# Two heads of a pair, one after the other or by turns: the order of half-width matmuls in a two-block transformer step

## The chip, the core and the metric

The kernel is one program on one NeuronCore of a Trainium2 chip. The metric is the device time of one execution in microseconds (us). The kernel before takes 2046.39 us, the median of 3 runs (2043.55 to 2046.69). One execution was also taken down by the hardware profiler; all rows below come from it.

Five engines work side by side, each through its own list of instructions, and wait for one another through semaphores. TensorE (PE in the rows) multiplies matrices, VectorE (DVE), ScalarE (ACT) and GpSimd (POOL) do the rest, SyncE (SP) issues the DMAs of the weights. PEld is TensorE's weight load: a matmul instruction takes a stationary operand (loaded first) and streams a moving operand past it. All data here are fp32, and each fp32 matmul of the program shows up in the trace as two matmul records with a weight load each. They are called passes here: one matmul is two passes.

## The reference

Two blocks run in sequence on 256 tokens of width 1024. The first has two layers, with multi-head latent attention (8 heads, value width 64) beside a Fourier and a convolution branch, then an MLP. The second mixes an RWKV-7 branch (8 heads of 64), an S5 branch and a gated linear attention (GLA, 4 heads with keys of 64), then cross-attention and a gated MLP. The parts that matter here:

```
attention      o[h] = softmax(q[h] k[h]^T * scale) v[h]              h = 0..7, value width 64
GLA            u_c = (k * exp(b_last - b))^T v, o = mask(q k^T) v + q S     4 heads, chunks of 64 tokens
RWKV-7 step    S = S*w + (S . -kk) (kk*a)^T + v k^T;  y = S . r             8 heads, state 64x64
```

The kernel computes RWKV in chunks of 64 tokens: per head and chunk, products of 64x64 blocks and the inverse of a unit triangular 64x64 block (built up from products), then a chain over the four chunks.

## The kernel before, in words

**Halves.** Everything is stored with features on the 128 partitions. A head is 64 wide, so a pair of heads fills the partitions: head 2i sits on partitions 0 to 63 (`hh = 0`), head 2i+1 on 64 to 127 (`hh = 1`). A product of one head therefore uses half of TensorE's array. A 64x64 block matmul reads partitions 0-63 and writes 0-63 of a PSUM bank, or reads 64-127 and writes 64-127. Values times probabilities of the attention (`pv`) reads all 128 partitions (keys) and writes only 64.

**The order.** The program is written out by hand; each engine follows the order of the code. PSUM has 8 banks. `open_bank` takes the next of a pool in turn and waits until the engine that read its last contents has freed it. `taken(pe, key)` makes TensorE wait for that reader, `did(..., key=...)` is its signal.

**Attention** (TensorE's part from line 706). Steps go over (pair i, head hh, query tile qt). In layer 0 there are 4 query tiles of 128, two with 256 keys and two with 512, so 32 steps; in layer 1 there are 2 tiles, both with 512 keys, so 16 steps. In step j TensorE computes the scores of j; DVE takes the maximum, ACT the exponential, DVE the reciprocal, and POOL scales the probabilities (line 1582). Three steps later (LAG = 3) TensorE transposes them (line 719), ACT copies the result to one of 3 slots of `probT` (line 1312), and one step after that TensorE multiplies values by probabilities: 2 or 4 matmuls of 64 columns of weights with 128 moving columns. In layer 0, TensorE also computes modulation blocks in between (`mod_block`, weights of 32 columns, each k in another quarter of the partitions of one bank).

**GLA** (from line 887): transposes of the values of each head (`gvt`), block products (`blocks`, line 896) and the updates `gu`, between projection tiles of the RWKV branch.

**RWKV** (from line 1020): `product(name, lhs, rhs)` (line 1027) calls `blocks` for each half of the four pairs: 2 halves of a name, 16 matmuls of 64x64 each, first the 8 of `hh = 0` and then the 8 of `hh = 1`. There are 21 products after the block transposes `vt`. Between them stand gate tiles (`gate_tiles`, 8 full matmuls each), which need nothing from the chain. DVE or ACT copies each half out. Then comes the chain over 4 chunks, `rx`, `ru`, a gate tile, `rs`, `ry`: TensorE waits for DVE after `rx` (line 2152), `ru` and `rs` (line 2164).

Of the kernel before, what the change touches and what calls it, by code (L numbers as in the profile page):

```python
# [27 lines left out]
P = 128  # L28
# [22 lines left out]
CHUNK = 64  # L51
# [21 lines left out]
LAG = 3  # L73
# [208 lines left out]
def two_blocks(nc, weights, vectors, table_in, x_in, ctx_in, mem_in, c_in, s5b_in, s5c_in, out):  # L282
# [3 lines left out]
    with ExitStack() as ctx:  # L286
# [228 lines left out]
        def steps(l):  # L515
            q_tiles = range(4) if l == 0 else range(2, 4)
            return [(i, hh, qt) for i in range(HEADS // 2) for hh in range(2) for qt in q_tiles]
# [18 lines left out]
        def _(pe):  # L536
# [91 lines left out]
            for l in range(LAYERS):  # L628
# [71 lines left out]
                for j in range(len(todo) + LAG + 1):  # L700
# [23 lines left out]
                    if 0 <= j - LAG - 1:  # L724
                        t = j - LAG - 1
                        i, hh, qt = todo[t]
                        key = ("pv", l, i)
                        if t % (len(todo) // 4) == 0:
                            open_bank(key, "hold")
                            if t == 0:  # L730
# [156 lines left out]
            for i in range(2):  # L887
                key = ("gvt", i)
                o_ = open_bank(key)
                for hh in range(2):  # L890
                    for c in range(NCH):
                        mm(o_[64 * hh:64 * hh + 64, c * P:(c + 1) * P], g_v[:, 2 * i + hh, c * CHUNK:(c + 1) * CHUNK],
                           table("ident"), True, True, key if hh == 1 and c == NCH - 1 else None)
            pe.wait_ge(S["gla_dve"], 3)

            def blocks(key, lhs, rhs, tiles, skip=()):

                o_ = open_bank(key)
                for hh in range(2):
                    hp = slice(64 * hh, 64 * hh + 64)  # L900
                    for n, i in enumerate(tiles):
                        for c in range(NCH):
# [10 lines left out]
            for i in range(2):  # L913
                taken(pe, ("gvt", i))
                key = ("gu", i)
                o_ = open_bank(key)
                for hh in range(2):
                    hp = slice(64 * hh, 64 * hh + 64)
                    for c in range(NCH - 1):
                        mm(o_[hp, c * P:(c + 1) * P], g_ket[hp, i, c * CHUNK:(c + 1) * CHUNK], g_vt[hp, i, c, :], True, True,  # L920
                           key if hh == 1 and c == NCH - 2 else None)
# [157 lines left out]
            def heads():  # L1079
                for hh in range(2):  # L1080
                    for i in range(4):
                        yield slice(64 * hh, 64 * hh + 64), i, hh == 1 and i == 3
            for c in range(NCH):
# [5 lines left out]
                for hp, i, end in heads():  # L1089
                    oo = o_[hp, 64 * i:64 * i + 64]  # L1090
                    if c:
                        mm(oo, r_kk[hp, i, cc], r_s[hp, i, :], True, False)
                    mm(oo, r_m2[hp, i, cc], r_vt[hp, i, cc], c == 0, True, key if end else None)
# [3 lines left out]
                for hp, i, end in heads():  # L1097
                    mm(o_[hp, 64 * i:64 * i + 64], c_tt[hp, i, cc], r_x[hp, i, :], True, True, key if end else None)
                gate_tiles(1)
                taken(pe, ("ru", c))  # L1100
                if c < NCH - 1:
                    key = ("rs", c)
                    o_ = open_bank(key)
                    for hp, i, end in heads():
                        oo = o_[hp, 64 * i:64 * i + 64]
# [4 lines left out]
                for hp, i, end in heads():  # L1110
                    oo = o_[hp, 64 * i:64 * i + 64]
                    if c:
                        mm(oo, r_s[hp, i, :], r_rt[hp, i, cc], True, False)
                    mm(oo, r_u[hp, i, :], r_n1[hp, i, cc], c == 0, False)
                    mm(oo, r_vt[hp, i, cc], r_n2[hp, i, cc], False, True, key if end else None)
# [1218 lines left out]
```

How the kernel before makes its waits and increments, by code:

```python
        def finished(eng, key):  # L476
            b, n = plan[key]
            eng.wait_ge(bank_full[b], n)
# [1 line left out]
        def taken(eng, key):  # L481
            b, n = plan[key]
            eng.wait_ge(bank_free[b], n)
# [8 lines left out]
            def did(ins, name=None, key=None, wait=True):  # L493
                s = bank_free[plan[key][0]] if key is not None else S[name or order]
                at_key = ("bank", plan[key][0]) if key is not None else (name or order)
                ins.then_inc(s, 1)
                if wait:
                    if key is not None:
                        eng.wait_ge(s, plan[key][1])
                    else:
                        count[at_key] = count.get(at_key, 0) + 1
                        eng.wait_ge(s, count[at_key])
                elif key is None:
                    count[at_key] = count.get(at_key, 0) + 1
                return ins
# [13 lines left out]
        def s5_turned_back(eng, n):  # L519
            if n % 4 == 3:
                eng.wait_ge(S["s5_states_v"], (n + 1) // 4)
            else:
                eng.wait_ge(S["s5_states"], n + 1 - (n + 1) // 4)
# [10 lines left out]
        @block.tensor  # L535
# [6 lines left out]
            def open_bank(key, pool="run"):  # L542
                b = pools[pool][turn[pool] % len(pools[pool])]
                turn[pool] += 1
                if uses[b]:
                    pe.wait_ge(bank_free[b], uses[b])
                uses[b] += 1
                plan[key] = (b, uses[b])
                return ps[:, b, :]
# [423 lines left out]
            s5_in(0)  # L973
            s5_in(1)
            pe.wait_ge(S["s5_dve"], 4)
```

## Time and profile before

| | us |
|---|---|
| median of 3 runs | 2046.39 |
| profiled execution | 2042.25 |
| its span | 2040.1 |
| TensorE busy | 1919.9 (94% of the span) |
| DVE / ACT / POOL busy | 911.9 / 411.6 / 230.9 |
| TensorE's share of the chain that ended last | 82% |

The profiled execution lies 4.1 us under the median. The stages that the change touches are the attention of layer 0 (180 to 289 us of the span) and of layer 1 (844 to 889), the GLA products (1228 to 1263), and the RWKV products and chain (1450 to 1625). The granted clock of TensorE is 0.964 of full speed on average.

### The profile page before, as it was taken

The page shows a single profiled execution, that of the slowest core. Times are in us where ns is not written, and L with a number is a line of the kernel's source. Part 1 is how long each engine was busy: PE and PEld are TensorE (multiplying, and loading weights), DVE is VectorE, ACT ScalarE, POOL GpSimd, SP SyncE. Part 2 cuts the span into 40 slices and gives each one's busy share as a digit, 9 for nine tenths or more (in the row PEclk, how much of TensorE's full clock was granted, in tenths as well). Part 3 has the DMA queues.
Part 4 walks back from the last instruction along what each step waited for, and adds up shares of the span by engine and source line. Part 5 has one row for each costly group of instructions (what it writes and reads, how often), then busy time and mean ns, then how long its engine had stood idle before and what let it go on. Part 6 is the DMA issues. An engine that isn't in the chain of part 4 may idle for free.

```text
span 2040.1 us, 26345 instructions
## 1 busy us (share of the span) xinstructions
PE 1919.9 (94%) x10716; PEld 1511.7 (74%) x10716; DVE 911.9 (45%) x1729; ACT 411.6 (20%) x778; POOL 230.9 (11%) x244
## 2 busy tenths in 40 slices
PE   6998999899999998999999899788999989999997
PEld 2444554788888886578999788544898878788886
DVE  1364322645754337637865312755610152245521
ACT  3124441320121103542210022102211001210000
POOL 0002420121012000322410000342000000000000
PEclk8999999999999999999999999887899999999999
DMA  8642641123332222124444542232212144244443
GB/s 314 256 186 106 260 174 62 63 101 105 124 104 83 83 83 104 42 85 143 166 165 164 176 152 94 76 103 105 82 43 84 42 165 145 83 145 145 161 149 103
DMA packets 38417, 256.23 MB, mean 126 GB/s; under 512 B 4097, under 2 KB 7169, under 8 KB 8609
## 3 DMA queue, kind: packets, MB, share of 16 engines
q1 hardware_dynamic: 35808, 239.80, 33.7%
q0 software_dynamic: 1920, 10.62, 1.4%
q10 hardware_dynamic: 576, 4.19, 0.5%
q8 instruction: 85, 1.39, 0.3%
q14 instruction: 28, 0.22, 0.0%
HBM read 247.26 MB, written 7.34 MB: 125 GB/s over the span
## 4 chain that ended last, share of the span: by engine, by line
PE 82%; DVE 10%; ACT 3%; issue 2%; DMA 1%; POOL 1%; SPq 0%; ACTq 0%; DVEq 0%; POOLq 0%
PE ps L567 82%; DVE arena L1779 1%; DVE arena L1935 1%; PE ps L719 1%; DMA cs_raw<-c_t 0%; DVE aux L1807 0%; DVE arena L1808 0%; DVE arena L1809 0%; ACT hT L1239 0%; DVE spare L2059 0%; ACT aux L1215 0%; DMA kept_keys_values<-arena 0%; DMA ring<-weights 0%; DVE aux L1722 0%; DVE aux L1718 0%
## 5 line engine op out<-in xcount | busy, mean ns | idle before, releaser
L567 PE MATMUL ps<-hT,ring 128*128 128x256 f32 (+3 forms) x3184 | 746.2, 393 | 24.0 <-issue 17.0
L567 PEld LDWEIGHTS ps<-hT,ring 128*128 128x128 f32 (+1 forms) x3184 | 579.0, 195 | 172.3 <-issue 97.5
L567 PE MATMUL ps<-arena,ring 128*128 128x256 f32 (+3 forms) x1756 | 359.1, 360 | 5.7 <-DVE arena L1809 3.2
L567 PEld LDWEIGHTS ps<-arena,ring 128*128 128x128 f32 (+1 forms) x1756 | 296.2, 192 | 58.4 <-issue 15.2
L567 PE MATMUL ps<-arena,sums 128*128 128x256 f32 (+1 forms) x768 | 136.5, 327 | 1.3 <-DVE aux L1873 1.3
L567 PEld LDWEIGHTS ps<-arena,sums 128*128 128x128 f32 x768 | 118.2, 191 | 12.3 <-DVE aux L1873 2.5
L567 PE MATMUL ps<-arena 64*64 64x64 f32 (+3 forms) x1392 | 92.7, 241 | 3.0 <-DVE arena L2111 1.6
L567 PEld LDWEIGHTS ps<-arena 64*64 64x64 f32 (+2 forms) x1392 | 86.6, 148 | 9.4 <-issue 6.4
L1193 ACT ACTIVATE aux<-xT 128x256 f32<-128x256 f32 (+1 forms) x64 | 30.9, 494 | 295.9 <-DVE xT L1965 98.6
L1582 POOL TENSOR_SCALAR aux<-aux,small 128x512 f32<-128x512 f32 (+1 forms) x48 | 71.3, 1491 | 152.9 <-DVE small L1825 152.9
L567 PE MATMUL ps<-hT,sums 128*128 128x128 f32 (+1 forms) x512 | 78.9, 302 | 0.7 <-DVE aux L1873 0.4
L567 PE MATMUL ps<-aux,tab 128*128 128x256 f32 (+1 forms) x156 | 59.3, 496 | 21.5 <-ACT aux L1193 17.7
L1849 DVE TENSOR_TENSOR sums<-ring 128x512 f32<-128x512 f32 x64 | 44.1, 690 | 71.5 <-PE ps L567 70.4
L1600 POOL TENSOR_TENSOR arena<-arena 128x256 f32<-128x256 f32 (+1 forms) x32 | 27.0, 844 | 426.9 <-ACT arena L1356 426.9
L1779 DVE SCALAR_TENSOR_TENSOR arena<-arena,vec 128x512 f32<-128x512 f32 (+1 forms) x120 | 73.6, 614 | 3.2
L567 PEld LDWEIGHTS ps<-hT,sums 128*128 128x128 f32 x512 | 70.1, 193 | 4.7 <-DVE aux L1873 0.8
L1818 DVE TENSOR_REDUCE small<-ps 128x1 f32<-128x512 f32 (+1 forms) x48 | 28.9, 602 | 99.6 <-PE ps L567 99.1
L1355 ACT ACTIVATE arena<-arena 128x1024 f32<-128x1024 f32 (+1 forms) x32 | 27.0, 844 | 209.8 <-DVE arena L1881 209.8
L1404 ACT ACTIVATE arena<-ps 128x512 f32<-128x512 f32 (+2 forms) x56 | 28.1, 501 | 181.6 <-PE ps L567 181.4
L567 PE MATMUL ps<-spare,ring 128*128 128x256 f32 x256 | 60.6, 379 | 1.3 <-DVE spare L1915 1.3
L567 PEld LDWEIGHTS ps<-aux,tab 128*128 128x128 f32 x156 | 29.4, 195 | 39.1 <-DMA cs_raw<-c_t 14.8
L567 PE MATMUL ps<-spare,sums 128*128 128x256 f32 x256 | 57.9, 379 | 0.0
(335 smaller groups left out, 2042.6 us busy)
## 6 DMA issues: line engine op xcount, KB each, us to landing
ring<-weights SPq DMA_DIRECT2D x224, 1024.0 KB, 4.9
kept_turns<-aux ACTq DMA_DIRECT2D x4, 1024.0 KB, 5.6
arena<-kept_turns POOLq DMA_DIRECT2D x6, 512.0 KB, 4.3
kept_keys_values<-arena POOLq DMA_DIRECT2D x1, 2048.0 KB, 6.6
arena<-kept_keys_values POOLq DMA_DIRECT2D x1, 2048.0 KB, 8.1
tab<-tables SPq DMA_DIRECT2D x1, 1411.5 KB, 10.9
xT<-ctx_t SPq DMA_DIRECT2D x1, 1024.0 KB, 6.0
xT<-x_t SPq DMA_DIRECT2D x1, 1024.0 KB, 8.2
```

The source lines that it names most:

```text
L567: ins = nc.tensor.matmul(o_, lhsT, rhs, start=start, stop=stop, skip_group_check=True)
L719: ins = nc.tensor.transpose(o_[:, kt * P:(kt + 1) * P], prob[:, t % 4, kt * P:(kt + 1) * P], table("ident"))
L1193: did(f(sq[:, k, s], xT[:, k, s], ACT.Square), "squares", wait=False)
L1355: did(f(two, two, ACT.Relu))
L1404: did(f(dst, bank(key)[0:m, 0:n], func, **kw), key=key, wait=wait)
L1582: did(nc.gpsimd.tensor_scalar(prob[:, t % 4, 0:nk], prob[:, t % 4, 0:nk], small[:, 3, t:t + 1], None, ALU.mult), "prob_ready", wait=False)
L1600: did(nc.gpsimd.tensor_tensor(t1, b12, b11, ALU.subtract))
L1779: did(v.scalar_tensor_tensor(dst, src, w, dst, ALU.mult, ALU.add), name)
L1818: did(v.reduce_max(small[:, 2, j:j + 1], bank(("s", l, j))[:, 0:nk], AX))
L1849: did(tt(s3, a11, a21, ALU.subtract))
L1935: did(v.reciprocal(a, a))
```

## The change

The same matmuls are issued, with the same operands and in the same number; only their order on TensorE changes.

- In `blocks`, `gvt`, `gu` and the RWKV chain the loop over the half moves inside, so that matmuls of partitions 0-63 and 64-127 alternate. In the chain, where a block is a sum of two or three products, the matmuls of one product alternate first, then those of the next. The group `go`, which writes all 128 partitions, stays.
- In the attention the steps go over (pair, query tile, head). Values times probabilities is done once for two steps, at the second, and its matmuls alternate between the two heads.

```diff
-            return [(i, hh, qt) for i in range(HEADS // 2) for hh in range(2) for qt in q_tiles]
+            return [(i, hh, qt) for i in range(HEADS // 2) for qt in q_tiles for hh in range(2)]
...
-                    if 0 <= j - LAG - 1:
-                        t = j - LAG - 1
-                        i, hh, qt = todo[t]
+                    t = j - LAG - 1
+                    if t >= 0 and t % 2 == 1:
+
+                        i, _, qt = todo[t]
...
+                        taken(pe, ("t", l, t - 1))
                         taken(pe, ("t", l, t))
-                        last = t % (len(todo) // 4) == len(todo) // 4 - 1
                         for kt in range(key_tiles(qt)):
-                            h = 2 * i + hh
                             end = kt == key_tiles(qt) - 1
-                            mm(o_[64 * hh:64 * hh + 64, qt * P:(qt + 1) * P], vtok[:, kt, h * DV:(h + 1) * DV],
-                               probT[:, t % 3, kt * P:(kt + 1) * P], kt == 0, end, key if last and end else None)
+                            for hh in range(2):
+                                h = 2 * i + hh
+                                mm(o_[64 * hh:64 * hh + 64, qt * P:(qt + 1) * P], vtok[:, kt, h * DV:(h + 1) * DV],
+                                   probT[:, (t - 1 + hh) % 3, kt * P:(kt + 1) * P], kt == 0, end,
+                                   key if t % per == per - 1 and end and hh else None)
...
             def blocks(key, lhs, rhs, tiles, skip=()):
 
                 o_ = open_bank(key)
-                for hh in range(2):
-                    hp = slice(64 * hh, 64 * hh + 64)
-                    for n, i in enumerate(tiles):
-                        for c in range(NCH):
-                            cc = slice(c * CHUNK, (c + 1) * CHUNK)
+                for n, i in enumerate(tiles):
+                    for c in range(NCH):
+                        cc = slice(c * CHUNK, (c + 1) * CHUNK)
+                        for hh in range(2):
+                            hp = slice(64 * hh, 64 * hh + 64)
...
-                    for hp, i, end in heads():
-                        oo = o_[hp, 64 * i:64 * i + 64]
-                        mm(oo, r_a2t[hp, i, cc], r_u[hp, i, :], True, False)
-                        mm(oo, r_k2t[hp, i, cc], r_vt[hp, i, cc], False, True, key if end else None)
+                    for i in range(4):
+                        v_ = slice(64 * i, 64 * i + 64)
+                        for hp in half_rows:
+                            mm(o_[hp, v_], r_a2t[hp, i, cc], r_u[hp, i, :], True, False)
+                        for hp in half_rows:
+                            mm(o_[hp, v_], r_k2t[hp, i, cc], r_vt[hp, i, cc], False, True,
+                               key if i == 3 and hp is half_rows[1] else None)
```

`gvt`, `gu`, `rx`, `ru` and `ry` are changed in the same way.

The order on TensorE in the attention of layer 1, three steps before; `spare,arena` are scores, `tab,aux` transposes, `aux,arena` values times probabilities of one head:

```order
L567 MATMUL ps<-spare,arena 128x512
L719 MATMUL ps<-tab,aux 128x128 x4
L567 MATMUL ps<-aux,arena 64x128 x4
L567 MATMUL ps<-spare,arena 128x512
L719 MATMUL ps<-tab,aux 128x128 x4
L567 MATMUL ps<-aux,arena 64x128 x4
```

And four steps of the changed kernel at the same place:

```order
L567 MATMUL ps<-spare,arena 128x512
L719 MATMUL ps<-tab,aux 128x128 x4
L567 MATMUL ps<-spare,arena 128x512
L719 MATMUL ps<-tab,aux 128x128 x4
L567 MATMUL ps<-aux,arena 64x128 x8
L567 MATMUL ps<-spare,arena 128x512
```

The four matmuls after each step's transposes have become eight after every second step's.

In the RWKV chain, on TensorE at the start of `rs` of the first chunk, before; `rinv,spare` is a2t times u, `spare` is k2t times v, both of one head:

```order
L567 MATMUL ps<-hT,ring 128x256 x8
L567 MATMUL ps<-rinv,spare 64x64
L567 MATMUL ps<-spare 64x64
L567 MATMUL ps<-rinv,spare 64x64
L567 MATMUL ps<-spare 64x64
```

And now:

```order
L567 MATMUL ps<-hT,ring 128x256 x8
L567 MATMUL ps<-rinv,spare 64x64 x2
L567 MATMUL ps<-spare 64x64 x2
L567 MATMUL ps<-rinv,spare 64x64 x2
L567 MATMUL ps<-spare 64x64 x2
```

The x2 is one matmul for each half. Where both products have the same names, as in `blocks`, the rows read alike before and after and are not shown.

## Rows read from the trace of the kernel before

**Rows 1.** The page: busy time, granted clock in 40 slices, the chain that ended last.

```profile
PE 1919.9 (94%) x10716; PEld 1511.7 (74%) x10716; DVE 911.9 (45%) x1729; ACT 411.6 (20%) x778; POOL 230.9 (11%) x244
...
PEclk8999999999999999999999999887899999999999
...
PE 82%; DVE 10%; ACT 3%; issue 2%; DMA 1%; POOL 1%; SPq 0%; ACTq 0%; DVEq 0%; POOLq 0%
```

**Rows 2.** Matmul groups by shape: busy us, mean ns; idle time before, releaser.

```profile
L567 PE MATMUL ps<-arena 64*64 64x64 f32 x1248 | 68.2, 230 | 1.6 <-DVE arena L2111 1.6
...
L567 PE MATMUL ps<-aux,arena 128*64 128x128 f32 x320 | 45.6, 283 | 1.5 <-ACT aux L1312 1.5
```

**Rows 3.** TensorE in time, attention of layer 1: start us, us, instructions merged.

```profile
859.72 1.12 PE L567 MATMUL ps<-spare,arena 96*128 96x512 f32 x2
860.68 0.60 PE L719 MATMUL ps<-tab,aux 128*128 128x128 f32 x4
861.21 1.09 PE L567 MATMUL ps<-aux,arena 128*64 128x128 f32 x8
862.23 1.13 PE L567 MATMUL ps<-spare,arena 96*128 96x512 f32 x2
```

**Rows 4.** TensorE in time, attention of layer 0.

```profile
222.60 0.65 PE L567 MATMUL ps<-aux,arena 128*64 128x128 f32 x4
223.18 1.13 PE L567 MATMUL ps<-spare,arena 96*128 96x512 f32 x2
224.24 1.92 PE L567 MATMUL ps<-ring,cs 128*32 128x512 f32 x16
...
286.68 0.63 PE L719 MATMUL ps<-tab,aux 128*128 128x128 f32 x4 [0.33 <-POOL aux L1582]
```

**Rows 5.** POOL in time, attention of layer 1.

```profile
864.63 1.72 POOL L1582 TENSOR_SCALAR aux<-aux,small 128x512 f32<-128x512 f32 x1 [0.80 <-DVE small L1825]
```

**Rows 6.** Counts of matmul records in two stretches of `gvt`: one stream, then two.

```profile
1227.94:1228.16 0.22, 0.22 (x4) 1.00 0.00 0
1228.27:1228.49 0.22, 0.22 (x7) 1.00 0.94 112
```

**Rows 7.** TensorE in time, GLA: `gvt`, a projection tile, `gu`, a projection tile.

```profile
1227.68 2.57 PE L567 MATMUL ps<-tab,arena 128*64 128x128 f32 x32
...
1233.51 10.63 PE L567 MATMUL ps<-hT,ring 128*128 128x256 f32 x48
...
1244.07 1.79 PE L567 MATMUL ps<-arena 64*64 64x128 f32 x24
1245.79 10.63 PE L567 MATMUL ps<-hT,ring 128*128 128x256 f32 x48
```

**Rows 8.** TensorE in time, RWKV products and gate tiles.

```profile
1455.32 11.10 PE L567 MATMUL ps<-arena 64*64 64x64 f32 x128 [1.64 <-DVE arena L2111]
1466.36 5.13 PE L567 MATMUL ps<-hT,ring 128*128 128x256 f32 x16
1471.41 6.42 PE L567 MATMUL ps<-arena 64*64 64x64 f32 x128
1477.76 3.72 PE L567 MATMUL ps<-hT,ring 128*128 128x256 f32 x16
```

**Rows 9.** TensorE in time, where product `m2` ends and `a2t` begins.

```profile
1484.48 0.22 PE L567 MATMUL ps<-arena 64*64 64x64 f32 x1
1484.54 0.22 PE L567 MATMUL ps<-tab,arena 64*64 64x64 f32 x1
1484.54 0.22 PE L567 MATMUL ps<-arena 64*64 64x64 f32 x1
1484.60 0.22 PE L567 MATMUL ps<-tab,arena 64*64 64x64 f32 x1
```

**Rows 10.** TensorE in time, RWKV chain: `rx` of the third chunk, then `ru`.

```profile
1599.74 0.28 PE L567 MATMUL ps<-rinv,arena 64*64 64x64 f32 x2
1599.85 0.28 PE L567 MATMUL ps<-spare 64*64 64x64 f32 x2
...
1601.71 1.12 PE L567 MATMUL ps<-rinv,arena 64*64 64x64 f32 x16 [0.59 <-DVE rinv L2152]
```

**Rows 11.** Busy us by engine, then granted clock, DMA share, GB/s.

```profile
1456.00:1466.00 10.00, 10.00 (x120) 10.00 (x120) 3.46 (x5) 0.00 (x0) 0.00 (x0) 0.50 0.01 3
```

**Rows 12.** ACT and DVE copying halves of products out of PSUM.

```profile
1494.86 0.60 ACT L1404 ACTIVATE spare<-ps 128x512 f32<-128x512 f32 x1 [0.91 <-PE ps L567]
...
1523.42 0.69 DVE L2140 TENSOR_TENSOR arena<-ps,tab 128x512 f32<-128x512 f32 x1 [14.79 <-PE ps L567]
```

More of the change, by code:

```diff
@@ L723, in _ @@
                         mod_turn(1, MOD_STEP[j])
-                    if 0 <= j - LAG - 1:
-                        t = j - LAG - 1
-                        i, hh, qt = todo[t]
+                    t = j - LAG - 1
+                    if t >= 0 and t % 2 == 1:
+                        i, _, qt = todo[t]
                         key = ("pv", l, i)
-                        if t % (len(todo) // 4) == 0:
+                        per = len(todo) // 4
+                        if t % per == 1:
                             open_bank(key, "hold")
-                            if t == 0:
+                            if t == 1:
                                 for tt in range(4):
@@ L898, in blocks @@
                 o_ = open_bank(key)
-                for hh in range(2):
-                    hp = slice(64 * hh, 64 * hh + 64)
-                    for n, i in enumerate(tiles):
-                        for c in range(NCH):
-                            cc = slice(c * CHUNK, (c + 1) * CHUNK)
+                for n, i in enumerate(tiles):
+                    for c in range(NCH):
+                        cc = slice(c * CHUNK, (c + 1) * CHUNK)
+                        for hh in range(2):
+                            hp = slice(64 * hh, 64 * hh + 64)
                             end = hh == 1 and i == tiles[-1] and c == NCH - 1
@@ L916, in _ @@
                 o_ = open_bank(key)
-                for hh in range(2):
-                    hp = slice(64 * hh, 64 * hh + 64)
-                    for c in range(NCH - 1):
+                for c in range(NCH - 1):
+                    for hh in range(2):
+                        hp = slice(64 * hh, 64 * hh + 64)
                         mm(o_[hp, c * P:(c + 1) * P], g_ket[hp, i, c * CHUNK:(c + 1) * CHUNK], g_vt[hp, i, c, :], True, True,
@@ L1076, in _ @@
                     taken(pe, (name, half))
[L1079 to L1082, printed above, removed]
+            half_rows = (slice(0, 64), slice(64, 128))
             for c in range(NCH):
@@ L1096, in _ @@
                 o_ = open_bank(key)
-                for hp, i, end in heads():
-                    mm(o_[hp, 64 * i:64 * i + 64], c_tt[hp, i, cc], r_x[hp, i, :], True, True, key if end else None)
+                for i in range(4):
+                    for hp in half_rows:
+                        mm(o_[hp, 64 * i:64 * i + 64], c_tt[hp, i, cc], r_x[hp, i, :], True, True,
+                           key if i == 3 and hp is half_rows[1] else None)
                 gate_tiles(1)
@@ L1103, in _ @@
                     o_ = open_bank(key)
-                    for hp, i, end in heads():
-                        oo = o_[hp, 64 * i:64 * i + 64]
-                        mm(oo, r_a2t[hp, i, cc], r_u[hp, i, :], True, False)
-                        mm(oo, r_k2t[hp, i, cc], r_vt[hp, i, cc], False, True, key if end else None)
+                    for i in range(4):
+                        v_ = slice(64 * i, 64 * i + 64)
+                        for hp in half_rows:
+                            mm(o_[hp, v_], r_a2t[hp, i, cc], r_u[hp, i, :], True, False)
+                        for hp in half_rows:
+                            mm(o_[hp, v_], r_k2t[hp, i, cc], r_vt[hp, i, cc], False, True,
+                               key if i == 3 and hp is half_rows[1] else None)
                 key = ("ry", c)
                 o_ = open_bank(key)
-                for hp, i, end in heads():
-                    oo = o_[hp, 64 * i:64 * i + 64]
+                for i in range(4):
+                    v_ = slice(64 * i, 64 * i + 64)
                     if c:
-                        mm(oo, r_s[hp, i, :], r_rt[hp, i, cc], True, False)
-                    mm(oo, r_u[hp, i, :], r_n1[hp, i, cc], c == 0, False)
-                    mm(oo, r_vt[hp, i, cc], r_n2[hp, i, cc], False, True, key if end else None)
+                        for hp in half_rows:
+                            mm(o_[hp, v_], r_s[hp, i, :], r_rt[hp, i, cc], True, False)
+                    for hp in half_rows:
+                        mm(o_[hp, v_], r_u[hp, i, :], r_n1[hp, i, cc], c == 0, False)
+                    for hp in half_rows:
+                        mm(o_[hp, v_], r_vt[hp, i, cc], r_n2[hp, i, cc], False, True,
+                           key if i == 3 and hp is half_rows[1] else None)
             gate_tiles(1)
```

4 lines of the change are left out of this document (2 added, 2 removed).

## The prediction

> **What bounds the kernel now.** I read the page first: TensorE is busy 94% of the span and makes 82% of the chain that ended last [rows 1]. So what TensorE no longer does comes off the time, unless a wait takes its place. Then the groups by shape: the change touches the 64x64 block matmuls and the 64-column ones of the attention, and TensorE is idle before either for less than 2 us in all [rows 2]. The sums below use start-to-start distances from the timeline, because a record's length (230 or 283 ns) holds a pipeline tail that the next record overlaps.
>
> What matters is the pace of one pass in a half of the array. In the attention of layer 1, 8 passes of values times probabilities take 862.23 - 861.21 = 1.02 us [rows 3]; in layer 0, 4 passes take 0.58 [rows 4]. The difference is 0.44 for 4 passes, so 0.109 us per pass and 0.15 us to get in and out. For 64x64 blocks, where two operands alternate in one half, 2 passes take 0.115 us [rows 10], so 0.058 per pass. But 128 passes of two products take 1477.76 - 1471.41 = 6.35 us, only 0.050 each [rows 8]. Where one product ends and the next begins, the records say why: passes of `arena` (the old, partitions 64-127) and `tab,arena` (the new, partitions 0-63) start in the same 0.06 us [rows 9]. The two halves run side by side, but only near a change of half. A run of 128 passes changes half 7 times. All in one line it would be 128 x 0.058 + 0.14 = 7.6 us; 6.35 is 1.26 less, 0.18 (three passes) at each of the 7. Three changes alone, those to another bank, would have given 7.06, so the overlap exists within a bank too. For columns alone `gvt` shows it: 4 records in 0.22 us, then 7 in 0.22 us [rows 6]; and the modulation block, four strips of 32 columns in one bank, does 16 passes of 512 columns in 1.92 us [rows 4], while a pass of 512 alone takes about 0.43 (two of them and a change make 1.13, of which the change is some 0.1 and the tail 0.16 [rows 3]).
>
> **The change part by part.** It removes no matmul. It lets each pass of one half find its partner of the other beside it all the time, since about three waiting passes are looked past and a partner is now at most two behind.
>
> *Attention, layer 1.* Two steps now hold two groups of 8 passes, 2.04 us. Afterwards one group of 16 passes in 8 slots: 8 x 0.109 + 0.15 = 1.02. Saved 1.02 for each of 8 pairs: 8.2 us. The next engine is POOL with 1.72 us per step [rows 5] against 2.51 of TensorE (862.23 - 859.72 = 2.51 [rows 3]); TensorE's step becomes 2.0, so POOL keeps hidden.
>
> *Attention, layer 0.* 8 pairs of long tiles at 1.02 and 8 of short ones at 0.58: 12.8 us. The steps go by tile now, so four short ones follow each other; the modulation blocks lie at the same steps, at least one in any three, and cover the probabilities' chain.
>
> *Tails.* The last transposes of layer 0 already wait 0.33 us for POOL [rows 4], so what is saved between the last scores and there turns into waiting: half of the 16 passes in between and a bit, 1.1 us. Layer 1 has no such wait but some 0.5 us of reserve; I take 0.5 lost. Attention in sum: 8.2 + 12.8 - 1.6 = 19.4 us.
>
> *GLA.* `gvt` with the two `blocks` behind it takes from 1227.68 to 1233.51, 5.83 us for 32 passes with 128 moving columns and 64 with 64 [rows 7]. Afterwards 16 x 0.109 + 32 x 0.058 + 0.35 for the changes = 3.95: 1.9 saved. `gu` goes from 1.72 (1245.79 - 1244.07) to 12 x 0.109 + 0.15 = 1.46: 0.3 saved. Nothing waits there. 2.1 us.
>
> *`vt`.* TensorE waits 1.64 us for DVE (line 2111) right behind it [rows 8]; what `vt` saves (1.2) lengthens this wait. 0.
>
> *Products.* Ten runs of 128 passes, each followed by a gate tile, and one of 64. A run becomes 64 x 0.058 + 0.14 = 3.9: 2.47 saved, ten times, and 1.3 for the short one: 26.0 us. The first run goes at a granted clock of 0.50 [rows 11], the level of 1.2 GHz, and takes 11.04 us (1466.36 - 1455.32 [rows 8]); in slots of 0.107 it is 7.1 or so, which gives 0.9 more than counted, taking part of the first gate tile into account. Against that stand new waits. A product half now comes every 0.95 us instead of 1.5, and 0.43 + 0.60 us pass from its end until ACT has copied it, 0.49 + 0.69 for DVE. The copy of `k2t`'s second half begins at 1494.86, that half ending at 1494.43 [rows 12]. A product that reads the one directly before it starts its first half when that copy is done, 0.95 after the end of the half: `d2` after `k2t` waits some 0.2, `r` after `d8` and `tt` after `ft` some 0.35 each. 0.9 lost. The copies themselves (0.60, 0.69) fit in 0.95. In sum 26.0 us.
>
> *Chain.* 448 passes. Where TensorE waits at the end (after `rx` of 32 passes, three times) the last pass comes 0.75 sooner, after 16 passes 0.28 sooner (`rx` once, `ru` four times); `rs` saves 0.57 three times and `ry` 0.75 once and 1.04 three times: 2.25 + 1.4 + 1.7 + 3.9 = 9.2 us. The wait of 0.59 for line 2152 [rows 10] is latency and stays.
>
> *Sum.* 19.4 + 2.1 + 0 + 26.0 + 9.2 = 56.7 us. The profiled execution takes 2042.25, its span 2040.1 and 2.15 around it; it goes to 1985.5. It lies 4.1 under the median of the runs, 2046.39, so the median goes to 1989.7. I say 1989.5.
>
> **A rule against it.** The Trainium skill, TensorEngine Tiling (Array Packing), section Restrictions and Gotchas, says that different row tiles write to different PSUM banks and cannot use one bank at the same time. The changed blocks let both halves write one bank, on other partitions. By that rule the two halves would have to run one after the other, and the 64x64 parts would get slower than now. The trace disagrees so far: the 6.35 us of a run need overlap at the changes within a bank too. It shows three passes at a time, not a steady stream, so the rule has its chance in the second rival.
>
> **Rivals.**
>
> *A. The passes are not fed fast enough (10%).* The longest stretch that the trace shows holds 0.050 us per pass, weight load included [rows 8]; the change wants 0.029. If the supply ended at 0.050, columns alone would gain (19.4 + 0.9, their pace is 0.055 per pass): 2046.4 - 20.3 = 2026. With a supply of 0.040 about half of the other 36 us remains: 2008. For it: no long stretch is faster. Against it: near each change two passes start every 0.058. The skill's TensorE: Matmul & The Clock Gate (section Wait — 56ns, not 53.3ns?) gives a floor of about 25 ns from start to start however small the matmul. That floor would leave all of the sum, 0.029 being above it.
>
> *B. Alternating halves run in line (4%).* If overlap needs some rest (another bank, or a half that has just drained), every pass costs its own 0.058: 1920 passes at 0.058 instead of 0.050 are 15 us more, and values times probabilities saves only its 24 ways in and out, 3.6: about 2058. If each turn also costs the unhidden first load (the first record of a run is 0.27 long, the others 0.22 [rows 9, 8]), 960 turns at 0.05 bring 48 more: about 2106. It decides from the point where a turn costs more than the three passes of overlap, 0.18, spread over 8 matmuls. Against it: rows 6 and 9.
>
> *C. The clock (4%).* The first product run and its gate tile go at 0.50 [rows 8, 11]. The engine had waited 1.64 us before. Shorter bursts between the same waits of the chain could bring more such stretches; 10 to 20 us at half pace cost 5 to 10: 1997. It can also go the other way: if a denser stream is granted full clock sooner, the 16 us from 1455 shrink by up to 6: 1984.
>
> *D. The attention keeps its pace (2%).* POOL, DVE's taps or the weights of the modulation blocks become the bound: half of 19.4 goes, 1999.
>
> **How the numbers follow.** The forecast holds 80%, with its own range of 1980 to 2000 for the waits and the clock. To leave out no more than 2 in 10 the range takes in the sooner clock and the half-way of A: 1976 to 2012. About 0.2% can be told from no change here. Faster by more than that are the forecast, A, C and D: 96%. B has the rest: no change 1%, where a partial overlap just meets the lost pace, slower 3%.
>
> **What would show it.** In the profile after: in layer 1 a group of 16 `aux,arena` passes per two steps from start to start 1.0 us, and 4.0 us for two steps; after each gate tile 128 passes in 3.9 us; `gu` in 1.5; the wait for line 2111 longer (2.8 us); new waits of 0.2 to 0.4 us on ACT line 1404 and DVE line 2140 between products; the stages 180 to 289, 844 to 889 and 1450 to 1625 shorter by about 12, 8 and 35 us. Runs of 128 passes that take over 5 us would prove A or B; the same runs at full pace with a granted clock of 0.50 over more than 25 us of that stage, C.

## The result, and the profile after

The changed kernel takes 1988.51 us, the median of 4 runs (1983.68 to 1990.18), against 2045.3 (2043.55 to 2046.69) for the kernel before in the same session: a ratio of 0.9719, 95% interval 0.9699 to 0.9739. A second set of runs gave 1985.36 and 0.9706 (0.9688 to 0.9724). The forecast was 1989.5 us, the ratio that it stood for 0.972.

The page of the profiled execution, answering to [rows 1]:

```profile
span 1981.5 us, 26361 instructions
...
PE 1850.5 (93%) x10716; PEld 1447.1 (73%) x10716; DVE 911.4 (46%) x1729; ACT 411.2 (21%) x778; POOL 230.4 (12%) x244
...
PE 81%; DVE 11%; ACT 3%; issue 2%; DMA 1%; POOL 1%; SPq 0%; ACTq 0%; DVEq 0%; POOLq 0%
```

TensorE has as many instructions as before, is busy 69.4 us less and still makes four fifths of the chain that ended last. The groups by shape, answering to [rows 2]:

```profile
L567 PE MATMUL ps<-arena 64*64 64x64 f32 x1248 | 40.5, 223 | 3.0 <-DVE arena L2124 3.0
...
L567 PE MATMUL ps<-aux,arena 128*64 128x128 f32 x320 | 22.9, 280 | 8.7 <-ACT aux L1325 8.7
```

One record is hardly shorter than before (223 ns for 230, 280 for 283), but the busy time of both groups falls by 41 to 50%, as passes of the two halves lie side by side. The third column holds the one surprise: before the groups of values times probabilities TensorE now waits 8.7 us for ACT's copy of the transposes (line 1325, line 1312 before), where it waited 1.5.

TensorE in time at the RWKV products (answers to [rows 8]):

```profile
1440.96 5.18 PE L567 MATMUL ps<-arena 64*64 64x64 f32 x128 [2.97 <-DVE arena L2124]
1446.08 3.72 PE L567 MATMUL ps<-hT,ring 128*128 128x256 f32 x16
1449.73 3.95 PE L567 MATMUL ps<-arena 64*64 64x64 f32 x128
1453.61 3.72 PE L567 MATMUL ps<-hT,ring 128*128 128x256 f32 x16
...
1487.56 4.09 PE L567 MATMUL ps<-arena 64*64 64x64 f32 x128
1491.58 3.72 PE L567 MATMUL ps<-hT,ring 128*128 128x256 f32 x16
```

A run of 128 passes goes from 6.35 us to 1453.61 - 1449.73 = 3.88, or 30 ns per pass. The run that holds a product reading the one just before it takes 1491.58 - 1487.56 = 4.02. The wait ahead of the first run is 2.97 us, as `vt` gets done sooner and DVE (line 2124) doesn't.

And in the attention of layer 1 (answers to [rows 3]), with ACT in the same stretch below it:

```profile
856.27 1.09 PE L567 MATMUL ps<-aux,arena 128*64 128x128 f32 x16 [0.89 <-ACT aux L1325]
857.30 1.12 PE L567 MATMUL ps<-spare,arena 96*128 96x512 f32 x2
858.26 0.60 PE L719 MATMUL ps<-tab,aux 128*128 128x128 f32 x4
858.70 1.02 PE L567 MATMUL ps<-spare,arena 96*128 96x512 f32 x2
859.56 0.60 PE L719 MATMUL ps<-tab,aux 128*128 128x128 f32 x4
861.05 1.09 PE L567 MATMUL ps<-aux,arena 128*64 128x128 f32 x16 [0.89 <-ACT aux L1325]
```

```profile
859.50 0.69 ACT L1317 ACTIVATE aux<-ps,small 128x512 f32<-128x512 f32 x1 [1.88 <-DVE small L1832]
860.09 0.19 ACT L1317 ACTIVATION_READ_ACCUMULATOR aux<-ps,small 128x1 f32 x1
860.31 0.60 ACT L1325 ACTIVATE aux<-ps 128x512 f32<-128x512 f32 x1
861.00 0.69 ACT L1317 ACTIVATE aux<-ps,small 128x512 f32<-128x512 f32 x1
```

The group of 16 passes takes the forecast 1.03 us (857.30 - 856.27). But two steps take 861.05 - 856.27 = 4.78 us and not 4.0. The transposes that line 1325 copies at 860.31 had been written by 858.86. ACT ran its work in the order of the code here, and ahead of that copy the code has the exponential of a later step (line 1317, at 859.50), which waits for DVE's maximum of scores that TensorE has only just computed. DVE at that place:

```profile
858.53 0.69 DVE L1831 TENSOR_REDUCE small<-ps 128x1 f32<-128x512 f32 x1 [1.82 <-PE ps L567]
859.25 0.15 DVE L1832 TENSOR_SCALAR small<-small 128x1 f32<-128x1 f32 x1
```

So the way from TensorE through DVE and ACT back to TensorE is: scores from 857.30, maximum at 858.53, exponential at 859.50, copy at 860.31, values times probabilities at 861.05, in all 3.75 us. TensorE's own work in that time is 2.86 us (861.05 - 857.30 - 0.89). In the kernel before a group of 1.02 us more lay in it, so that way stayed hidden.

The time by stages, in us of the span. A stage's half-clock time is in brackets: how long the granted clock stood at 0.50, the level of 1.2 GHz, within it. "Attention" ends where TensorE goes on to something else; "RWKV products" begin with `vt`. The second profiled execution of the changed kernel is shown too.

| stage | before | after | after, again | forecast of the gain |
|---|---|---|---|---|
| up to the first scores | 180.6 | 182.2 | 182.0 | 0 |
| attention, layer 0 | 108.4 (3.4) | 99.9 (10.2) | 97.9 (3.4) | 11.7 |
| between the attentions | 555.6 | 559.6 | 555.6 | 0 |
| attention, layer 1 | 43.9 (3.4) | 39.6 (0) | 40.4 (3.4) | 7.7 |
| up to `gvt` | 339.2 | 338.8 | 339.3 | 0 |
| GLA products | 17.9 | 15.7 | 15.7 | 2.1 |
| S5, up to `vt` | 204.7 (61.4) | 200.1 (47.8) | 206.8 (64.9) | 0 |
| RWKV products | 125.8 (13.7) | 95.4 (3.4) | 95.7 (3.4) | 26.0 |
| RWKV chain | 48.4 (10.2) | 35.6 (3.4) | 35.7 (3.4) | 9.2 |
| rest | 415.6 | 414.5 | 414.6 | 0 |

Between the two executions of the same program only the clock differs, by 4 us between the attentions and by 6.7 in S5. Against the second, whose clock in the attention is that of before, the gain is 10.5 + 3.5 there, 2.2 in GLA and 42.8 in RWKV; the other stages are 2.5 us longer in sum (S5 by 2.1, with 3.5 us more at half clock), which makes the 56.5 us between the spans (2040.1 and 1983.6).

Two things stand to be explained: 5.4 us that the attention didn't give (14.0 for 19.4), and 7.6 us that RWKV gave beyond its 35.2.

### The profile page after: what moved, and what is told of

It is laid out like the page before. It is cut to its first block, busy times and chain, and to the rows that moved or that the text cites. A ratio compares the mean times of both kernels' runs of the same rounds, so it can differ in the third digit from the quotient of the medians.

```text
span 1981.5 us, 26361 instructions
## 1 busy us (share of the span) xinstructions
PE 1850.5 (93%) x10716; PEld 1447.1 (73%) x10716; DVE 911.4 (46%) x1729; ACT 411.2 (21%) x778; POOL 230.4 (12%) x244
## 3 DMA queue, kind: packets, MB, share of 16 engines
q1 hardware_dynamic: 35808, 239.80, 34.8%
## 4 chain that ended last, share of the span: by engine, by line
PE 81%; DVE 11%; ACT 3%; issue 2%; DMA 1%; POOL 1%; SPq 0%; ACTq 0%; DVEq 0%; POOLq 0%
PE ps L567 80%; DVE arena L1792 1%; DVE arena L1948 1%; DMA ring<-weights 1%; DVE small L1831 1%; DMA cs_raw<-c_t 0%; DVE aux L1820 0%; DVE arena L1821 0%; DVE arena L1822 0%; ACT hT L1252 0%; ACT aux L1228 0%; PE ps L719 0%; DVE spare L2072 0%; DMA kept_keys_values<-arena 0%; POOL aux L1595 0%
## 5 line engine op out<-in xcount | busy, mean ns | idle before, releaser
L567 PE MATMUL ps<-arena 64*64 64x64 f32 (+3 forms) x1392 | 63.6, 233 | 4.3 <-DVE arena L2124 3.0
L567 PEld LDWEIGHTS ps<-arena 64*64 64x64 f32 (+2 forms) x1392 | 57.5, 143 | 10.9 <-issue 6.4
L567 PE MATMUL ps<-spare,ring 128*128 128x256 f32 x256 | 61.4, 383 | 2.1 <-DVE spare L1928 2.1
L567 PEld LDWEIGHTS ps<-aux,tab 128*128 128x128 f32 x156 | 30.4, 201 | 40.3 <-DMA cs_raw<-c_t 14.7
L1888 DVE TENSOR_TENSOR aux<-aux,ps 128x256 f32<-128x256 f32 x24 | 10.1, 421 | 106.8 <-PE ps L567 106.6
```

Of the source, the lines that this page charges most:

```text
L567: ins = nc.tensor.matmul(o_, lhsT, rhs, start=start, stop=stop, skip_group_check=True)
L1888: did(tt(u2, p1, product("p6"), ALU.add))
```

## The experiments

### Each part alone

`attn_only` is the kernel before with the change of the attention, `blocks_only` has the other part (blocks, `gvt`, `gu`, chain). `after_again` is the changed kernel, for a second time. In the two cuts of code, minus lines are those of the changed kernel and plus lines those of the kernel named.

```diff
--- attn_only against after
-                for n, i in enumerate(tiles):
-                    for c in range(NCH):
-                        cc = slice(c * CHUNK, (c + 1) * CHUNK)
-                        for hh in range(2):
+                for hh in range(2):
+                    for n, i in enumerate(tiles):
+                        for c in range(NCH):
...
--- blocks_only against after
-            return [(i, hh, qt) for i in range(HEADS // 2) for qt in q_tiles for hh in range(2)]
+            return [(i, hh, qt) for i in range(HEADS // 2) for hh in range(2) for qt in q_tiles]
...
```

> Only the attention part of the change; blocks, gvt, gu and chain in the order of before. My theory: the attention saves what the two profiles show, about 8.5 us in layer 0 and 2 to 4 in layer 1, because TensorE waits for ACT's copy of the transposes (line 1312) some 0.9 us before each double group in layer 1. So 2033 to 2036 us. The pass pace in a double group is 0.055 us or less. Rival, the prediction's sizes: 19.4 us, 2026. If the MLP behind it slows down because the attention got denser, less than 8 us remain and the MLP stretch between the two attentions is 4 us longer than before.

Measured: 2034.1 us, ratio 0.9943 (0.9921 to 0.9965). This median describes no run: of the 8, four took 2027.7 to 2028.6 us at a mean granted clock of 0.964, and four 2039.6 to 2041.0 at 0.956 or 0.957. Only one of the first four was profiled, so in which stage the others lost their 12 us is open. That 2034.1 lies within the expected 2033 to 2036 is luck. In the profiled execution layer 0 takes 97.9 us and layer 1 40.4, all other stages what they take in the kernel before, within 0.6; its attention saves 14.0 us, more than the 10.5 to 12.5 expected.

> Only the 64x64 blocks, gvt, gu and the chain alternate; attention as before. My theory: 37 us by the sum of slots (2.1 GLA, 26.0 products, 9.2 chain) and up to 8 more where the stretch of halved clock at the start of the products does not appear: 2000 to 2008 us. A run of 128 passes takes 3.88 us. Rival: the 8 us more are not of the clock but of the blocks themselves; then the stage from vt to the chain's end takes 131 us even in a profile that shows a granted clock of 0.5 there.

Measured: 2000.02 us, ratio 0.9768 (0.9751 to 0.9784). GLA 15.7, RWKV products 95.8, chain 35.6, the attention as before (108.4 and 44.0). The time is at the lower end of the expected 2000 to 2008.

> The changed kernel again, on the chip and in the rounds of the three others. 0.972 of before. A stretch of halved clock of 3.4 us at the start of the RWKV products if its length goes with the order of the blocks, anything between 0 and 14 us if it is chance.

Measured: 1985.36 us, with the half-clock stretch of 3.4 us. The parts add up in the spans of the profiled executions: 2040.1 - 2025.6 = 14.5 us for the attention and 2040.1 - 1998.0 = 42.1 for the rest make 56.6, the whole has 2040.1 - 1983.6 = 56.5. (The ratios of the medians add up as well, 0.0057 + 0.0232 = 0.0289 for 0.0294, but the first of them is that of no run.) So the parts don't disturb one another, and the attention's shortfall is its own: 97.9 and 40.4 us stand in `attn_only` too.

### What the attention waits for

Theory: ACT's order. The copy of the transposes stands behind an exponential that isn't due yet, and TensorE's shorter step lays that bare. `act_first` puts the copy first (but for layer 0's steps with a modulation block). `pv_later` leaves ACT alone and does the double group one step later, ahead of the transposes of that step, so that the copy has a step more. Rival: another engine (POOL, or DVE) sets the step, and the copy only shows it.

```diff
--- act_first, ACT's part of one step
-                    if j < len(todo):
-                        ...
-                        did(f(prob[:, j % 4, 0:nk], bank(("s", l, j))[:, 0:nk], ACT.Exp, ...), key=("s", l, j))
                     ...
                     if j >= LAG:
                         t = j - LAG
                         nk = key_tiles(todo[t][2]) * P
                         finished(act, ("t", l, t))
                         did(f(probT[:, t % 3, 0:nk], bank(("t", l, t))[:, 0:nk], ACT.Copy), key=("t", l, t))
+                    if not mods_here:
+                        exps()
--- pv_later, TensorE's part of one step (the transposes now come behind this)
-                    t = j - LAG - 1
+                    t = j - LAG - 2
                     if t >= 0 and t % 2 == 1:
                         ...
```

> The changed kernel, with ACT copying the transposes before it takes the exponential of the same step (except in steps with a modulation block). My theory: the wait before the double group came from the copy standing behind the exponential, so it vanishes in layer 1 (5.7 us over 7 times) and in the steps of layer 0 without a modulation block; two steps take 4.0 to 4.1 us instead of 4.78; 5 to 8 us faster than the changed kernel, 1981 to 1984. Rival: POOL and DVE bind at 2.3 us per step anyway; then the wait moves to POOL line 1582 and no more than 2 us come of it.

> The changed kernel, with values times probabilities one step later, ahead of that step's transposes; ACT's order is unchanged. My theory: there are then 3.97 us of TensorE's work between the scores and the group that needs the copy behind them, against 3.8 us of chain, so the wait for ACT goes as well, and two steps take 4.0 us in layer 1; 5 to 8 us faster than the changed kernel, less some 1 us at the end of each layer. Rival: as for act_first, POOL binds at 2.3 us per step.

Measured: `act_first` 1983.34 us, ratio 0.9689 (0.9671 to 0.9707); `pv_later` 1978.95 us, 0.9667 (0.9651 to 0.9684). The changed kernel has 0.9706 (0.9688 to 0.9724), which `act_first` still overlaps and `pv_later` just doesn't. By these ratios the gains are 3.5 and 8.0 us, where 5 to 8 were expected of either (of `pv_later` less 1 for its ends). `act_first` falls short by its ratio, though its 1983.34 lies within the expected 1981 to 1984; its profile has 8.5 us more at half clock in layer 0 than `pv_later`. What decides is the stage and the wait itself. TensorE in time in layer 1, first of `act_first`, then of `pv_later`:

```profile
855.70 1.09 PE L567 MATMUL ps<-aux,arena 128*64 128x128 f32 x16
856.72 1.12 PE L567 MATMUL ps<-spare,arena 96*128 96x512 f32 x2
857.68 0.60 PE L719 MATMUL ps<-tab,aux 128*128 128x128 f32 x4
858.12 1.02 PE L567 MATMUL ps<-spare,arena 96*128 96x512 f32 x2
858.99 0.60 PE L719 MATMUL ps<-tab,aux 128*128 128x128 f32 x4
859.52 1.09 PE L567 MATMUL ps<-aux,arena 128*64 128x128 f32 x16
```

```profile
848.77 1.09 PE L567 MATMUL ps<-aux,arena 128*64 128x128 f32 x16
849.80 0.66 PE L740 MATMUL ps<-tab,aux 128*128 128x128 f32 x4
850.29 1.02 PE L567 MATMUL ps<-spare,arena 96*128 96x512 f32 x2
...
852.55 1.09 PE L567 MATMUL ps<-aux,arena 128*64 128x128 f32 x16
```

And POOL in `pv_later`, the scaling of the probabilities:

```profile
848.82 3.47 POOL L1595 TENSOR_SCALAR aux<-aux,small 128x512 f32<-128x512 f32 x2 [0.51 <-DVE small L1838]
852.59 3.25 POOL L1595 TENSOR_SCALAR aux<-aux,small 128x512 f32<-128x512 f32 x2 [0.30 <-DVE small L1838]
```

Two steps are 859.52 - 855.70 = 3.82 us in the one and 852.55 - 848.77 = 3.78 in the other. The wait on ACT's copy is gone between these steps in both; over the whole kernel it falls from 8.7 us to 1.9 and 2.0. POOL does its two steps in 3.25 to 3.47 us and still idles between them, though only for 0.3 to 0.5. So the rival falls: no other engine held the step at 4.78. In this table, us of the stage, in brackets the half-clock time, then TensorE's idle time in it:

| | layer 0 | idle | layer 1 | idle |
|---|---|---|---|---|
| before | 108.4 (3.4) | 7.6 | 43.9 (3.4) | 2.6 |
| after, again | 97.9 (3.4) | 11.8 | 40.4 (3.4) | 7.7 |
| act_first | 99.2 (11.9) | 9.9 | 36.6 (3.4) | 4.2 |
| pv_later | 93.5 (3.4) | 8.6 | 34.8 (0) | 4.0 |
| both | 93.1 (3.4) | 8.1 | 36.1 (3.4) | 3.9 |

With the wait out of the way the attention gives 24.0 us (`pv_later`; 23.1 with both), more than the 19.4 forecast, with the stage's half-clock time 3.4 us less in the first and as before in the second. The forecast had allowed only 1.6 for tails and waits; it had no place for a way through another engine's order.

That the gain exceeds even the 21.0 us that the forecast had before tails has a second source. It put TensorE's own work of two steps at 5.02 - 1.02 = 4.0 us, and it is 3.8. Where scores now follow the transposes directly, they start 0.44 us after them (858.12 - 857.68) and the next transposes 0.87 after that; before, it was 0.53 from transposes to values and 0.96 from scores to transposes ([rows 3]). There are fewer changes of shape, and that is 0.18 us for each pair of steps, 1.4 in layer 1. The rest of the surplus wasn't taken apart.

`pv_later_act_first` has both edits, `before_act_first` only ACT's, on the kernel before.

> Both repairs of the attention: values times probabilities one step later, ahead of the transposes, and ACT's copy before its exponential. If the copy behind the exponential was all that was waited for, the second repair adds nothing over pv_later except up to 1 us at the ends of the layers: 1977 to 1979. If TensorE's wait then sits with POOL, the same. Rival: the two add up, 1974.

Measured: 1976.73 us, ratio 0.9664 (0.9646 to 0.9682), the same as `pv_later` within their intervals. The two edits remove one and the same wait. It is the fastest of all kernels run here by its median, 0.3 us under the expected 1977 to 1979, and `pv_later` can't be told from it.

> The kernel before, with only ACT's copy of the transposes put ahead of the exp of the same step, as in act_first. If that edit helps by itself, it gains here too, in the attention of both layers, about the 3 to 5 us that it gave beside the double group. If it only takes away the wait that the shorter step of TensorE laid bare (theory held), there is next to nothing to gain: TensorE's own work of two steps stays 5.02 us, its waits on ACT are 1.5 us in all, so at most 1.5 us less, 0.1%: 2044 to 2046 us, ratio 0.999 to 1.001.

Measured: 2048.36 us, ratio 1.0029 (1.0019 to 1.0039): no gain, a loss of 0.3%. The attention stages take 108.1 and 43.5 us, 0.7 less in sum, inside the forecast's 1.5. The loss lies elsewhere: the RWKV chain, whose code is that of before, takes 53.9 us instead of 48.4 with 23.9 us at half clock instead of 10.2. It is hardly a chance of one execution: all nine of this kernel have a mean granted clock of 0.958 to 0.961, the 19 of the kernel before in the same session 0.962 to 0.965 (in other sessions it had single ones down to 0.960). Why this edit should cost the chain its clock is open. In the attention the edit is worth something only where the change has made TensorE's step short, which is what the theory says.

### How far a partner may be away

The prediction took "about three waiting passes are looked past" from the kernel before. Two kernels alternate in coarser turns, after every 2 or 4 matmuls (4 or 8 passes) of a half. The kernel before alternates after 8 matmuls, the changed one after 1. Of the edit only the new loops are shown, for turns of 4; `groups2` has a 2 in both places.

```diff
+                todo_ = [(n, i, c) for n, i in enumerate(tiles) for c in range(NCH)]
+                for g0 in range(0, len(todo_), 4):
+                    for hh in range(2):
+                        hp = slice(64 * hh, 64 * hh + 64)
+                        for n, i, c in todo_[g0:g0 + 4]:
```

> The changed kernel, with blocks turning between the halves after every 4 matmuls (8 passes) instead of every one. My theory: TensorE starts a pass of the idle half if no more than three waiting passes stand before it. Then a half's group starts when the sixth pass of the other's runs, 16 passes take 10 slots of 0.058 and a run of 128 passes takes 4.7 to 4.8 us (3.88 in the changed kernel, 6.35 before): some 9 us slower than the changed kernel. Rival 1, that it looks far ahead and before was slow for another reason: 3.9 us. Rival 2, that overlap is a fixed three passes at each change: 16 changes per run less one, 7.6 - 15 x 0.18 = 4.9 us, close to mine; told apart by groups2.

> The changed kernel, with blocks turning between the halves after every 2 matmuls (4 passes). My theory (three waiting passes looked past): the other half's group starts when the second pass runs, and both halves stay busy: 3.9 to 4.0 us for 128 passes, no difference from the changed kernel. Rival, one that looks past fewer: then 4.4 us and more, 5 us slower in all.

Measured: `groups4` 1994.42 us, ratio 0.975 (0.9729 to 0.9771); `groups2` 1986.12 us, 0.971 (0.9689 to 0.9731). The same run of 128 passes, in `groups4`, then in `groups2`:

```profile
1454.52 4.99 PE L567 MATMUL ps<-arena 64*64 64x64 f32 x128
1459.44 3.72 PE L567 MATMUL ps<-hT,ring 128*128 128x256 f32 x16
```

```profile
1451.86 4.00 PE L567 MATMUL ps<-arena 64*64 64x64 f32 x128
1455.78 3.72 PE L567 MATMUL ps<-hT,ring 128*128 128x256 f32 x16
```

From start to start a run takes 6.35 us in turns of 8 matmuls, 4.92 in turns of 4, 3.92 in turns of 2 and 3.88 by ones. The prediction's formula, all in line less three passes of 0.058 at each change of half, gives 128 x 0.058 + 0.14 - 7 x 0.174 = 6.3 for turns of 8, from which it was made, and 7.56 - 15 x 0.174 = 4.95 for turns of 4, which is its one real test. With turns of 2 (31 changes) it would go below what side by side allows, 3.9, and this floor is what was measured; that shows no more than that at least the passes of such a turn overlap. The expectation for `groups4` has 4.7 to 4.8 us as its own theory and 4.9 as that of a rival, a fixed overlap at each change. The two are one count: 16 groups of 5 slots and 3 more for the last, which has no partner behind it, make 83 slots of 0.058 and 0.14, or 4.95. The 4.7 to 4.8 left out those 3. So nothing here tells a view ahead of three passes from a fixed overlap of three. By the time, `groups4` is 9.0 us slower than the changed kernel (0.975 against 0.9706), as expected. Turns of 2 matmuls can't be told from turns of 1 by the time: 0.971 lies within the intervals of the changed kernel.

The end of one product (`arena`, partitions 64-127) and the start of the next (`tab,arena`, partitions 0-63, in another bank) in `groups4` show the pairs at single records:

```profile
1465.39 0.27 PE L567 MATMUL ps<-tab,arena 64*64 64x64 f32 x1
1465.44 0.22 PE L567 MATMUL ps<-arena 64*64 64x64 f32 x1
1465.50 0.22 PE L567 MATMUL ps<-tab,arena 64*64 64x64 f32 x1
1465.50 0.22 PE L567 MATMUL ps<-arena 64*64 64x64 f32 x1
1465.55 0.22 PE L567 MATMUL ps<-tab,arena 64*64 64x64 f32 x1
1465.56 0.22 PE L567 MATMUL ps<-arena 64*64 64x64 f32 x1
```

Two passes, one of each half, start within the same 0.01 us, and the next pair 0.05 later. The first pass of the new half starts at 1465.39, ahead of three passes (1465.44, 1465.50, 1465.56) that stand before it in the code: these are the three.

### The clock at the start of the products

In both profiled kernels with the old block order (before and `attn_only`) the first product run lies in a stretch of 13.7 us at half clock. In all with alternating blocks the stretch is 3.4 us. Theory 1: the order of these passes makes the difference. Theory 2: chance, or the blocks further on. Two kernels mix the orders. (`groups4`, which takes turns of 4 matmuls, is among those with 3.4.)

```diff
--- first_old: the kernel after, but m1 and m1t half by half
+                alt_ = key[0] not in ("m1", "m1t")
--- first_new: the kernel before, but m1 and m1t by turns
+                alt_ = key[0] in ("m1", "m1t")
--- in both
+                order_ = [(hh, x) for x in todo_ for hh in range(2)] if alt_ else [(hh, x) for hh in range(2) for x in todo_]
```

> The kernel after, with only the first two products of the RWKV chunk stage (m1 and m1t, 256 of its 64x64 passes) in the old order, half by half. The question is the clock at the start of that stage: 13.7 us at half clock in both profiled kernels with the old block order everywhere, 3.4 us in every one with alternating blocks. Theory 1, the first lone-half passes bring the long stretch: the half-clock stretch near 1440 us is back at 10 us or more, the run of 128 passes of m1 takes 6.4 us and at half clock up to 11, and the stage from vt to the chain's end is 7 to 11 us longer than in the kernel after (about 138 to 142 us against 131.0 to 131.3): 2 x 2.5 us for the passes themselves and 3 to 5 us for the clock; in all +0.4 to +0.5% against the kernel after. Theory 2, the stretch came and went by chance or by the later blocks: it stays at 3.4 us, the stage is 5 us longer or less (136 us).

> The kernel before, with only m1 and m1t (256 passes) in the alternating order. Theory 1 (the lone-half passes of the stage's start bring the long half-clock stretch): the stretch of 13.7 us near 1456 us falls to 3.4 us or moves to a later run of lone-half passes; if it goes, the stage from vt to the chain's end is 174.2 - 5 - 5 = about 163 to 166 us. Theory 2 (chance, or the later blocks): a stretch of 10 us or more stays and the stage is 169 us or more.

Both expectations count 256 passes for the two names. That was a slip: `m1` and `m1t` are one run of 128, so the passes themselves are worth 2.5 us, not 5.

Measured: `first_old` 1992.1 us, ratio 0.9752 (0.9738 to 0.9765), against 0.9706 (0.9688 to 0.9724) for the changed kernel. Its first run and gate tile:

```profile
1442.07 10.89 PE L567 MATMUL ps<-arena 64*64 64x64 f32 x128 [2.96 <-DVE arena L2127]
1452.89 5.35 PE L567 MATMUL ps<-hT,ring 128*128 128x256 f32 x16
1458.18 3.95 PE L567 MATMUL ps<-arena 64*64 64x64 f32 x128
```

The half-clock stretch is back at 13.7 us, behind the same wait of 2.96 us. The products take 102.7 us instead of 95.7: 7.0 more. Of these 2.5 are the passes at full clock (6.35 - 3.88), so 4.5 are left for the clock. The stage up to the chain's end takes 138.3 us, within the 138 to 142 of theory 1.

`first_new`: 2040.08 us, ratio 0.9985 (0.9976 to 0.9994). The stretch falls from 13.7 to 3.4 us, and the products take 118.8 us instead of 125.8, the same 7.0. Columns of the rows below: the stretch, its length, busy us of PE, PEld, DVE, ACT and POOL with their records, then the granted clock, DMA share, GB/s. The second part of the stretch, first in the kernel before, then in `first_new`:

```profile
1459.10:1469.30 10.20, 10.20 (x93) 9.54 (x93) 3.54 (x6) 0.00 (x0) 0.00 (x0) 0.50 0.01 2
```

```profile
1459.30:1469.40 10.10, 10.10 (x175) 9.34 (x172) 4.53 (x7) 0.38 (x1) 0.00 (x0) 1.00 0.31 105
```

TensorE is busy without a gap in both. What differs is what it did just before: lone halves or pairs. Over all 13 profiles the split is clean: 13.7 us in the four whose first run goes half by half, 3.4 in the nine where it goes by turns.

But the stage as a whole missed: 172.8 us, where theory 1 said 163 to 166 (about 167 without the slip) and theory 2 had 169 or more. The chain, with unchanged code, takes 54.0 us instead of 48.4, at half clock for 23.9 us instead of 10.2, as it does in `before_act_first`; that is 5.6 of the miss. In the old order the chain's clock goes either way (10.2 us in two profiles, 23.9 in two); in the new order it was 3.4 us in all nine profiles of it. Theory 1 holds for the products, in both directions. Why the old chain sometimes loses its clock isn't settled.

## Why the prediction was right, and where it was not

- **The bound and the formula** held: TensorE's passes were the time, and 64 slots of 0.058 + 0.14 came out as 3.88 us per run for 3.9. Rival A (supply) falls with 0.030 us per pass, rival B (in line) with it. The rows that spoke against B ([rows 6, 9]) were the ones to trust: they show at a change of half what now goes on all the time. (The first record of 0.27 us that the prediction counts for B stands in neither of the rows it names; in `groups4` it stands at 1465.39.)
- **The rule against it.** The rule of the Trainium skill (TensorEngine Tiling (Array Packing), Restrictions and Gotchas), that two row tiles cannot use one PSUM bank at the same time, doesn't hold for these blocks: both halves write one bank, on other partitions, and 32 passes into one bank take a quarter of the 3.88 us, 0.030 each, where one half alone needs 0.058. In the run at 1449.73 two passes start 0.01 us apart, and two more every 0.06.
- **Products** 26.0: 30.4 or 30.1 measured. Without the 4.5 us of clock that `first_old` and `first_new` show, 25.6 remain. The prediction had counted 0.9 for a first run that stays slow throughout, and put a sooner clock at up to 6 us in its range only (rival C, the other way). This is what came true.
- **New waits between products** 0.9: smaller. The run of `d8` and `r` takes 4.02 us for 3.88, 0.14 more and not 0.35.
- **Chain** 9.2: 12.8 measured, with 6.8 us less at half clock. At half pace that is 3.4 us, which leaves 9.4. That part is worked out, not shown by a run of its own.
- **GLA** 2.1: 2.2. **`vt`** 0, with the wait at 2.97 for a forecast 2.8.
- **Attention** 19.4: 12.8 and 14.0. The step that failed is "TensorE's step becomes 2.0, so POOL keeps hidden": two steps take 4.78 us in layer 1 and not 4.0, 0.89 of it a wait for ACT. It asked whether another engine has too much work per step, and none has. It didn't ask how long it takes from one TensorE instruction to a later one through DVE and ACT in their order: 3.75 us, against 2.86 of own work. The rows to see it in were those of ACT, where line 1312 stands right behind an exponential. The wait of 1.5 us on that line in [rows 2] was a hint that the reserve was small. Rival D, at 2%, had the attention lose half of its gain (9.7; 5.4 were lost), but named POOL, DVE's taps and the weights, and `act_first` and `pv_later` show ACT's order instead. The term had a second error the other way: without the wait the attention gives 23.1 to 24.0.
- **The sum** was right within 1 us in part by luck: 5.4 us less in the attention stand against 7.6 more in RWKV, most of it clock.

## What to carry to other kernels

Matmuls that use half of the array should alternate between the halves. For the 64x64 fp32 blocks here turns of one or two matmuls were enough: about three passes overlap at a change of half, so turns of 8 left 2.5 of 6.4 us. After a step of the bounding engine is made shorter, add up every round trip through the other engines' queues and set it against the new step; their busy shares don't tell. In an engine's program, put first what is ready (the copy), and then what waits (the exponential), or let the consumer come a step later. Here the later consumer did at least as well: 0.9667 against 0.9689.

## What the hardware showed beyond the forecast

- The granted clock went with what TensorE did, not only with whether it was busy. Behind a wait of 1.6 to 3.0 us, the same 128 passes half by half stay at half clock with the gate tile behind them, for 13.7 us; by turns they do so for 3.4. This is worth 4.5 us on top of the passes' own 2.5, in either direction.
- Two executions of one program differ by 4 us in a stage of 555 through such stretches alone, and in `attn_only` executions of one program fall into two groups 12 us apart, at 0.964 and 0.956 of the clock. A median over such runs, and a small difference between kernels, say little until the granted clock beside them is compared.
- A kernel can also be granted less clock in all its executions, in a stage that the edit doesn't touch: `before_act_first` is 0.3% slower than the kernel before although its own stages are 0.7 us shorter. The cause is open.
